# A decoder layer on Trainium2: first 128 tokens carried ahead through output projection and first queries, expert value products placed among the query blocks

## The reference

```
y_a = a_pre @ w_conv_out
y_b = attn_o @ w_attn_out
mix = sigmoid(g_a) * y_a + sigmoid(g_b) * y_b
x   = x + gate1 * (mix @ w_out)
h2  = modulate(rmsnorm(x, norm2_w), shift2, scale2)
q   = h2 @ w_q                       # 8 heads x 2 halves x 128
s   = q . sub_keys                   # 16 score rows of 128 keys
...                                  # top 16 of each half, top 16 of their 256 sums: expert numbers e
act = gelu(u_tab[e] . h2);  y = sum_k (softmax(top_s) * act)_k * v_tab[e]_k
out = x + gate2 * y
```

## Time and profile before

| what | value |
|---|---|
| median of 3 runs (lowest, highest) | 1151.59 us (1149.05, 1152.76) |
| the profiled execution | 1151.69 us |
| its span, first to last instruction | 1149.9 us |
| PE, DVE, ACT, POOL busy | 85%, 62%, 21%, 50% |
| DMA over the span | 379.89 MB, 330 GB/s |
| of it the gathers of u and v | 312.92 MB on the software queue, with the cache pages |
| first gather issued | 381.82 us |
| granted clock of TensorE, mean | 0.991 |

### The profile page before, as it was taken

The page is one execution under the profiler, slowest core; times in us unless marked ns, Lnnn a source line. Parts: engine busy times, 40 slices in busy tenths (PEclk is TensorE's granted clock), DMA queues, the critical chain, the costliest instruction groups (busy, mean ns, idle before and its releaser), DMA issues.

```text
span 1149.9 us, 10850 instructions
## 1 busy us (share of the span) xinstructions
PE 983.1 (85%) x3401; PEld 497.9 (43%) x3401; DVE 718.0 (62%) x1765; ACT 242.6 (21%) x593; POOL 575.2 (50%) x618
## 2 busy tenths in 40 slices
PE   6998889999999999998777777777777777778888
PEld 3456766667677874542232222222222222222333
DVE  2357466888644798768567467477576576444342
ACT  2111223113402133341112112121121021121111
POOL 0201001002000567777777777777777777777760
PEclk9999889999999999999999999999999999999999
DMA  9961423779537699999999999999999999999994
GB/s 314 351 221 57 152 74 129 256 256 286 148 120 287 245 345 382 409 408 410 409 409 409 409 410 409 409 409 410 410 409 409 410 409 410 409 410 409 409 411 179
DMA packets 123403, 379.89 MB, mean 330 GB/s; under 512 B 11612, under 2 KB 21080, under 8 KB 123348
## 3 DMA queue, kind: packets, MB, share of 16 engines
q0 software_dynamic: 86208, 312.92, 69.3%
q1 hardware_dynamic: 36966, 66.19, 16.7%
q10 hardware_dynamic: 174, 0.11, 0.1%
HBM read 377.59 MB, written 1.59 MB: 330 GB/s over the span
## 4 chain that ended last, share of the span: by engine, by line
PE 37%; DMA 28%; POOL 20%; issue 8%; DVE 6%; ACT 1%; SPq 0%; DVEq 0%; ACTq 0%; POOLq 0%
DMA big<-peer_v,oT 13%; POOL big L1060 9%; POOL big L1049 8%; PE twoA L567 7%; DMA big<-peer_u,oT 7%; PE twoA L880 5%; DMA r<-peer_u,oT 4%; PE twoD L935 4%; PE twoD L937 3%; PE twoD L821 3%; PE twoA L545 2%; POOL r L1049 2%; PE twoA L490 2%; PE twoD L809 1%; DMA big<-w_in 1%
## 5 line engine op out<-in xcount | busy, mean ns | idle before, releaser
L1049 POOL DMA_INDIRECT big<-peer_u,oT x230 | 216.5, 941 | 179.1 <-DVEq L1777 107.0
L1060 POOL DMA_INDIRECT big<-peer_v,oT x266 | 252.6, 950 | 87.5 <-issue 69.6
L1819 DVE CUSTOM_DVE_ANT_0 big<-big,twoA 128x1024 f32<-128x1024 f32 x128 | 156.2, 1221 | 143.5 <-DMA big<-peer_u,oT 142.5
L1819 DVE CUSTOM_DVE_ANT_0 big<-big,twoD 128x1024 f32<-128x1024 f32 x102 | 123.3, 1218 | 54.9 <-DMA big<-peer_u,oT 53.6
L935 PE MATMUL twoD<-big 128*128 128x512 f32 x176 | 97.0, 633 | 40.4 <-DMA big<-peer_v,oT 38.7
L567 PE MATMUL twoA<-hT,big 128*128 128x288 f32 x448 | 117.6, 419 | 0.0
L935 PE MATMUL twoD<-big,modT 128*128 128x512 f32 x132 | 73.1, 636 | 31.1 <-DMA big<-peer_v,oT 30.7
L567 PEld LDWEIGHTS twoA<-hT,big 128*128 128x128 f32 x448 | 86.2, 196 | 28.8 <-issue 5.9
L937 PE MATMUL twoD<-big 128*128 128x512 f32 x176 | 89.9, 592 | 0.0
L935 PEld LDWEIGHTS twoD<-big 128*128 128x128 f32 x176 | 27.5, 188 | 104.6 <-DMA big<-peer_v,oT 96.4
L935 PE MATMUL twoD<-big,rstd 128*128 128x512 f32 x90 | 49.9, 636 | 21.8 <-DMA big<-peer_v,oT 21.7
(11 more groups left out here) (368 smaller groups left out, 1419.0 us busy)
## 6 DMA issues: line engine op xcount, KB each, us to landing
big<-w_ada SPq DMA_DIRECT2D x12, 2048.0 KB, 8.3
big<-w_in SPq DMA_DIRECT2D x5, 2048.0 KB, 13.6
big<-w_in SPq DMA_DIRECT2D x9, 1024.0 KB, 7.6
big<-peer_w_q SPq DMA_DIRECT2D x3, 2048.0 KB, 8.8
big<-peer_v,oT POOLq DMA_INDIRECT x266, 18.5
big<-w_out SPq DMA_DIRECT2D x2, 2048.0 KB, 11.7
big<-peer_u,oT POOLq DMA_INDIRECT x230, 16.3
big<-w_conv_out SPq DMA_DIRECT2D x1, 2048.0 KB, 13.7
```

The lines of the kernel that those rows point to most:

```text
L1049: pool.indirect_dma_start(urows[i % NU], None, peer_u, bass.IndirectOffsetOnAxis(ap=eidx[:, t, s:s + 1], axis=0)).then_inc(u_in[i % NU], 16)
L1060: pool.indirect_dma_start(vrows[j % NV], None, peer_v, bass.IndirectOffsetOnAxis(ap=eidx[:, t, s:s + 1], axis=0)).then_inc(v_in[j % NV], 16)
L1819: dve.tensor_tensor_reduce(out=urows[i % NU], in0=urows[i % NU], in1=h2tok[t][:, :], scale=1.0, scalar=0.0, op0=ALU.mult, op1=ALU.add, acc ...
```

## The change

It reorders the second half of the mixer and the start of the expert stage.

- The first 128 columns go ahead alone. Their attention output projection stands between the sample's softmax transposes and value products (`attn_first`, 2 x 4 blocks of 128 columns, two instructions per block and k in the trace), four of their output blocks behind the value products, four behind the tail transposes, then two query blocks made together, k by k. The square sums are for 128 columns.
- The other 160 columns (`REST`) come after the first scores: `RESTS` cuts their 8 blocks in groups of 3, 3 and 2, which share PSUM banks of a new ring `R`. DVE mixes them (`rest_mix`) after `route(0)`, adds their residual at the dots 3, 6 and 8, and norms them after dot 12.
- PE makes query blocks 2 to 7 for the first 128 columns early, then 16 blocks (160 columns for the first eight, 288 for the others) with products between them: `SLOTS_BY` says how many products stand ahead of each block, 24 in all.
- The sigmoid is cut in four and stands between the key copies of ACT.
- The buffers are laid out anew: u has 6 buffers for the first 30 slots and 10 later, v has 4 for 16 slots, then 9, and 13 from slot 34 on, when the query weights are done. `w_out` goes to slots 1 and 5, the first query weights to 6. The lag grows from 14 to 20. `LATE` work moves 20 slots back.

The core of the diff (left out: the bodies that follow from the words above, such as `rest_residual`):

```diff
-        LAG, NEAR, LAST_NEAR = 18, 8, 4
+        LAG, NEAR, LAST_NEAR = 20, 14, 4
+        U_FIRST, U_ROWS = 30, 6
+        V_FIRST, V_ROWS, V_SOME = 16, 4, 34
...
-                ("out", cols(w_out, 0, 512), 5), ("out", cols(w_out, 512, 512), 6),
-                ("peerq", peer_cols(0), 5), ("peerq", peer_cols(1), 4), ("peerq", peer_cols(2), 0), ("peerq", peer_cols(3), 1)]
+                ("out", cols(w_out, 0, 512), 1), ("out", cols(w_out, 512, 512), 5),
+                ("peerq", peer_cols(0), 6), ("peerq", peer_cols(1), 4), ("peerq", peer_cols(2), 0), ("peerq", peer_cols(3), 1)]
...
         SUB_ORDER = (0, 2, 1, 3)
-        LATE = list(range(6, 6 + 2 * 15, 2))
+        LATE = list(range(26, 26 + 2 * 15, 2))
         H2_REST = 64
-        SCORE_AFTER = [4, 8, 12]
-        EARLY = {8: 0, 12: 1}
+        REST_AT, REST_NORM = (3, 6, 8), 12
+        RESTS = ((0, 3), (3, 6), (6, DC))
+        SLOTS_BY = [2 + j for j in range(8)] + [10 + 2 * j for j in range(8)]
+        SCORE_AFTER = {11: 3, 15: 4}
...
+        u_row = [i % U_ROWS if i < U_FIRST else (i - U_FIRST + U_ROWS) % NU for i in range(ROUNDS)]
+        v_some = (4, 0, 1, 2, 3, 5, 6, 7, 8)
+        v_all = (9, 10, 11, 12) + v_some
+        v_row = [j % V_ROWS if j < V_FIRST else v_some[(j - V_FIRST) % 9] if j < V_SOME else v_all[(j - V_SOME) % NV]
+                 for j in range(ROUNDS)]
+
...
+            attn_first(0)
             turn_probs(0)
             turn_probs(1)
+            attn_first(1)
             sample_values(0)
             sample_values(1)
+            pe.wait_ge(a_free, A.n)
+            sum_bank.append(bankA[(A.n + 3) % 4])
+            for j in range(4):
+                out_first(j)
...
+            for j in range(4, DC):
+                out_first(j)
...
+            first = weights(pe, group("peerq"))
+            pair = [A.open(pe) for _ in range(2)]
+            for k in range(DC):
+                pe.wait_ge(h_ready, DC + k + 1)
+                for j in range(2):
+                    mm = pe.matmul(pair[j][:, 0:P], first[:, k, j * P:(j + 1) * P], hT[:, k, 0:P], start=(k == 0), stop=(k == DC - 1))
+            A.close(mm, 2)
...
+            for j in (2, 3):
+                query(j, 0, P)
+            score_unit(1)
...
+            pe.wait_ge(oT_ready, 3)
+            w = weights(pe, group("attnout"))
+            for a, e in RESTS:
+                b = R.open(pe)
...
+                R.close(mm)
+            released[group("attnout")] = (r_full, R.n)
+            for n, (a, e) in enumerate(RESTS):
+                b = R.open(pe)
+                for j in range(a, e):
...
+                    for k in range(DC):
+                        if j == 0:
+                            pe.wait_ge(mix_ready, 3 if k < 3 else 4 if k < 6 else 5)
...
+                R.close(mm)
+            for j in (4, 5):
+                query(j, 0, P)
...
+            pe.wait_ge(sq_ready, 2 * DC + 3)
+            for c in range(DC):
...
+            rest_sum.append((a_full, A.n))
+            for j in (6, 7):
+                query(j, 0, P)
+            score_unit(2)
+            pe.wait_ge(r_free, R.n)
...
+            multiplied = 0
+            for j in range(16):
+                while multiplied < SLOTS_BY[j]:
+                    products(multiplied)
+                    multiplied += 1
+                if j == 0:
+                    pe.wait_ge(h_ready, 2 * DC + 1)
+                query(j, P if j < 8 else 0, TOK, ready=(j == 0))
+                if j in SCORE_AFTER:
+                    score_unit(SCORE_AFTER[j])
+            for j in range(multiplied, ROUNDS):
+                products(j)
...
-                if g == group("out"):
+                if g == group("out", 1):
...
                     sp.dma_start(conv_prompt, tailrows[0:2, :]).then_inc(conv_out_done, 16)
                     sp.dma_start(conv_sample.rearrange("b j c -> (b j) c"), tailrows[2:18, :]).then_inc(conv_out_done, 16)
-                if g == group("peerq", 1):
-
-                    sp.wait_ge(*released[group("out", 1)])
+                if g == group("peerq", 3):
...
+                before = row_before(u_row, i)
+                if before is not None:
+                    pool.wait_ge(u_used, before + 1)
+                elif u_row[i] >= U_ROWS:
                     pool.wait_ge(*released[group("peerq")])
-                if i >= NU:
-                    pool.wait_ge(u_used, i - NU + 1)
...
+                before = row_before(v_row, j)
+                if before is not None:
+                    pool.wait_ge(v_used, before + 1)
+                elif v_row[j] < 4:
+                    pool.wait_ge(*released[group("out", 1)])
                 else:
-                    pool.wait_ge(v_used, j - NV + 1)
...
+                    pool.wait_ge(*released[group("peerq", 1 if v_row[j] == 4 else 2 if v_row[j] < 9 else 3)])
...
-                lag = min(LAG, NEAR + 4 + i // 4, LAST_NEAR + (ROUNDS - 1 - i) // 2)
+                lag = min(LAG, NEAR + i // 6, LAST_NEAR + (ROUNDS - 1 - i) // 2)
...
+                part = sig[:, 4 * (bb - KB):4 * (bb - KB) + 4, :].rearrange("p j t -> p (j t)")
+                L.tell(act.activation(part, part, ACT.Sigmoid), gates_ready)
...
+            for j in (2, 3):
...
+            for n, (a, e) in enumerate(RESTS):
+                act.wait_ge(x1_ready, DC + n + 1)
+                L.tell(act.activation(sqR[:, a:e, :], xT[:, a:e, P:TOK], ACT.Square), sq_ready)
...
+            b = A.take(act)
+            L.tell(act.activation(rstd[:, P:TOK], b[:, 0:REST], ACT.Sqrt, bias=cv["eps"], scale=1.0 / D), sd_ready)
...
+            exps(0)
+            for j in (6, 7):
+                copy_query(j, 0, P)
+            gelus(0)
+            copy_scores()
+            act.wait_ge(h_scaled, 1)
+            for c in range(DC):
+                L.tell(act.activation(hT[:, c, P:SEQ], hT[:, c, P:SEQ], ACT.Identity, bias=modT[:, 24 + c, 0:1]), h_rest, wait=False)
...
+            made = 0
+            for j in range(16):
+                while made < SLOTS_BY[j]:
+                    diagonal(made)
+                    made += 1
+                copy_query(j, P if j < 8 else 0, TOK)
+                if j in EARLY_EXP:
+                    exps(EARLY_EXP[j])
+                if j in EARLY_GELU:
+                    gelus(EARLY_GELU[j])
+                if j in SCORE_AFTER:
+                    copy_scores()
+            for j in range(made, ROUNDS):
+                diagonal(j)
...
+            norm_scale(32, 56)
+            dve.wait_ge(gates_ready, 4)
+            dve.wait_ge(co_ready, CONV_FILL[0])
+            for i, conv_side in enumerate((bufX, bufC)):
+                L.tell(tt(sig[:, 4 * i:4 * i + 4, :], sig[:, 4 * i:4 * i + 4, :], conv_side, ALU.mult))
...
+                b = V.take(dve)
+                L.tell(dve.scalar_tensor_tensor(xT[:, j, 0:P], b[:, 0:P], modT[:, 16 + j, 0:1], xT[:, j, 0:P], ALU.mult, ALU.add),
+                       x1_ready)
+                free()
+                L.tell(ts(hT[:, j, 0:P], xT[:, j, 0:P], ab[:, j, 0:1], None, ALU.mult), wait=False)
...
+            R = Banks([bankD[0], bankD[1]], r_full, r_free)
+
+            def rest_mix(n):
+
+                a, e = RESTS[n]
+                mix(R.take(dve), a, e - a, P, TOK)
+                dve.sem_inc(r_free, 1)
...
+            for n in range(len(RESTS)):
+                rest_mix(n)
...
+                if i in REST_AT:
+                    rest_residual(REST_AT.index(i))
+                if i == REST_NORM:
+                    rest_norm()
+                if sum(chunks[weighed]) == (i + 1 if weighed >= LAST else i - 3 if weighed else i - 5):
...
+                if found < 3:
+                    steps = 2 if found == 1 or i > REST_NORM + 1 else 0
+                elif found == 3:
+                    steps = 2 if near <= 23 else 0
+                else:
+                    steps = 2 if near <= 26 else 1 if near < 44 else 0
+                for _ in range(steps):
                     if found < len(units) and next(router, True):
                         found += 1
                         router = route(found) if found < len(units) else iter(())
+                        if found <= 3:
+                            break
```

More of the change, by code:

```diff
@@ L886, in _ @@
-            score_unit(4)
+            for j in (2, 3):
[6 more added lines that the diff above has]
+                for j in range(a, e):
+                    for k in range(4):
+                        mm = pe.matmul(b[:, (j - a) * REST:(j - a + 1) * REST], w[:, k, j * P:(j + 1) * P], oT[:, k, P:TOK],
+                                       start=(k == 0), stop=(k == 3))
+                R.close(mm)
@@ L914, in late, with products @@
                     A.close(mm)
-            for j, (t, s) in enumerate(slots):
+            def products(j):
+                t, s = slots[j]
                 acc = bankD[2 * (t % 2):2 * (t % 2) + 2]
@@ L1249, in _ @@
             act.sem_inc(a_free, 1)
```

(19 more changed lines are left out.)

212 lines of the change are left out of this document (101 added, 111 removed).

## The result

The changed kernel takes 1175.2 us (median of 4 runs, 1174.0 to 1183.4), the kernel before, run beside it, 1152.0: a ratio of 1.022, with a 95% interval from 1.0195 to 1.025. It is slower, as forecast, and 8 us slower than the forecast of 1167.0: just past the 1158 to 1174 that had 0.65, and inside the 1153 to 1178 given for 8 in 10. The profiled execution took 1175.16 us, with a span of 1173.3.

What follows compares the result with a forecast made beforehand. Full DMA engines bound the kernel; a change moves only the stream's start and the idle before it is full. First gather 356.9 + idle 40 + weights 10.3 + gathers 738.4 + output 2.6 = 1148.2, forecast 1167.0 us, range 1158 to 1174 (0.65).

Steps and rivals of the forecast that it cites:

- rival C: SP's store blocks again for 8.39 us, so queries wait for weights to 350; 1175 us, chance 0.12.
- (1): Sigmoid among ACT's key copies: table load and two quarters hold up PE's first conv block by 3.8 us.
- (2): Attention projection in two halves of 3.55 us: transposes start at 309.2, second half ends at 314.9, value products at 319.4.
- (3): Output blocks, 1.78 us each plus 0.22 of square sum: four end at 327.1, four more at 336.0; first query 340.6.
- (4): SP's queue: stores issue in 0.5 us, first query weights issued at 333.0, landing 341.8; first queries start at 342.0.
- (5): First queries to first gather: 14.9 us, before 16.3; first gather at 356.9, 24.9 us earlier.
- To the first product: DVE's work between first gather and first product takes 42 us; first product at gather + 45, 16 u rows out before.
- sum 111: Query blocks, products, scores, hand-overs and table loads on PE take 111 us; last block ends at gather + 155.
- 36 + 4: DMA idle in the ramp: 36 us up to the last query block plus some 4 for refilling; 40, for 10.1 before.
- A: Faster: DVE and POOL keep the stream full, idle 10 us; 1137 us, decided at idle 25.4, chance 0.11.
- B: Half of it: idle 22 to 29 us, as hand-overs vanish or mixes fit in the first landing; near 1151, chance 0.07.
- D: TensorE's clock falls to 0.88 in the ramp, so 90 us of matmuls take 12 more; 1179 us, chance 0.05.

Runs made afterwards that it cites:

- e3: Changed kernel plus dummy work: PE multiplies constants in the two waits ahead of the first product; 1260.1 us, against 1265.1 for the changed kernel.
- e5: The changed kernel as it is, run again on what is taken to be another chip; 1265.1 us, ratio 1.024 to the kernel before.
- e2: Changed kernel with the four sigmoid quarters on ACT among the first conv copies, not the key copies; 1258.2 us, against 1265.1 for the changed kernel.

## Why the prediction was right, and what it mis-sized

The direction, the mechanism and most of the places hold; one term is too small by 8 us. That the time is also the 1175 of rival C, to 0.2 us, is chance: its mechanism didn't occur.

*The way to the first gather.* Forecast 356.9, measured 356.1. (1) The sample's scores start 4.2 us later on the chain (298.66 for 294.44 at their first long group), for 3.8. That agreement is in part luck. The first conv block starts 2.8 us later (282.82 for 280.04), although ACT's copies began 0.9 sooner (275.50 for 276.39), so the table load and two quarters cost 3.7 of the 3.8. The head start of 0.9 was in no term, and neither was a loss of 1.5: the conv blocks take 15.29 us for 13.82, at a lower clock.

Conv blocks after and before, by stretches:

```profile
282.82:298.10 15.28, 15.28 (x57) 11.50 (x58) 9.36 (x13) 6.52 (x11) 0.00 (x0) 0.90 0.82 213
280.04:293.86 13.82, 13.82 (x57) 10.56 (x58) 12.41 (x16) 4.18 (x9) 0.53 (x1) 1.00 1.04 234
```

PE had stood for 2.62 and 1.35 us just ahead of them (the wait that this step itself puts there), and the granted clock is 0.50 to 284 and 0.55 to 286. The Trainium skill (ScalarE: Activation LUTs, What ACT_TABLE_LOAD costs) would have had 5.2; ACT's row shows the activation 0.01 us behind the end of the load again, so its drain of 1.38 isn't seen here either. (2) The transposes start at 309.70 (309.2), the second half of the attention projection ends at 315.4 (314.9), the value products at 319.9 (319.4). (3) Four output blocks end at 327.5 (327.1), all eight at 336.0. (4) The query weights are issued at 332.33 (333.0) and land at 341.3 (341.8). (5) From the first queries to the gather it is 14.7 us (14.9). The stores take 0.99 and 0.98 us to issue, so rival C is out, and with it the 8.39 as a property of the store. Two halves of the attention projection were put at 0.111 us an instruction, an estimate that goes beyond its row; measured is 3.57 / 32 = 0.112.

*To the first product.* 44.4 us after the gather, for 45, and 17 u rows ahead of the first v for 16. DVE has the weights of the first product ready at 397.5, 41.5 after the gather, for 42; then ACT still has eight shifts of h2 (2.45) ahead of the diagonal. The chain runs there through the sum of squares at the low clock (386.64, 4.61 us, where e3 has 2.34 at a clock of 1.00), which no term had. So it is in part luck as well that this place comes out within a microsecond.

*The phase of query blocks.* This is the step that failed: "sum 111", the last block at gather + 155. It ends at gather + 163.0. From the timeline: blocks 8 x 2.19 + 8 x 3.89 = 48.6 (forecast 48.4), products 24 x 1.72 = 41.3 (41.3), scores 0.9 (1.9), gaps with their table loads 19.9 (19). Missing were two terms. A product behind a gap starts 0.24 us slower (1.10 for 0.86), 15 times: 3.6. And the clock: the first two products take 6.06 us for 3.68, one half product 1.48 for 0.86, one block 3.25 for 2.19, 4.1 together. The prediction had taken "two pieces of 0.86" from a product in the middle of others, though in its own schedule every block is followed by a product that starts behind a gap; the 1.10 of such a start stands in the earlier trace rows.

*The idle time.* The last of the 33 v and 54 u rows are asked by then, as forecast (87 issues up to 519). Forecast 36 + 4, measured 43.4 + 6.3: again the longer phase, and 2 in the refill, for which POOL stood 5.90 us behind the scores of the last block.

*The rivals.* A and B are out: idle 49.7, far from 25.4 (which by the prediction's own sum should be 40 - 15.3 = 24.7; nothing hangs on it). D named the right thing at the wrong size and for the wrong reason. It took the clock of a busy stretch with short gaps, 0.88, for the whole ramp, and priced 12 us. What happened is that PE stood for lack of input and ran at 1.2 GHz for a while after, in the phase (4.1 us), ahead of it (the sum of squares) and among the conv blocks (1.5); in e3, where PE hardly stood ahead of the first product, the clock stayed there. The Trainium skill (TensorE: Matmul & The Clock Gate, Part 1) ties the clock to how busy PE has been, and here the rows agree; the prediction held only the busy share of a stretch against it and not the two waits ahead of the first product, which its own step on DVE's 42 us implied.

*The signs to look for.* "DMA share near 0.75 between 357 and 512" was the wrong column: the share is 0.84 there, and the rate, 300 GB/s of 409 over 356 to 519, is 0.73. The stream is full from 535 (409 GB/s; 335 from 530 to 535), for 520.

## What to carry to other kernels

When a stream that is bound by transfers starts earlier, ask how much of other work the engine that frees its buffers must still do, and count what can be asked by the end of it: the time is the end of that work plus a nearly constant rest. There each hand-over between engines costs in full, several times over (the wait, a slower first instruction, a lower clock), so put what the next step needs in the queue ahead of what only has to be done some time. A price taken from the middle of a run of like instructions doesn't hold for one that stands alone.

## What the runs showed of the hardware

The first comparison and the later runs, by all signs on different chips of one kind, differ by 7% for this kernel: 1152 against 1231 to 1237 us for the kernel before, a full stream of 409 against 366 to 370 GB/s. In the later runs ACT, DVE and PE stand here and there for 1 to 7 us, once for 12, with their input there and nothing in the trace that they waited for (the copy at 509.80 above). This isn't scattered: e5, e3 and e2, on two chips, have the holes ahead of the same products, 7.72, 7.73 and 7.58 us, and 2.95, 2.94 and 3.00. On the first chip the same kernel has 1.11 at both places. Such stretches make an order that hands over late more expensive still. Their cause wasn't tried and stays open.

The issue of a small store on SP took 8.39 us in one kernel and 0.99 in the other, and that of the last two query weights 1.00 before and 13.41 once the gathers had begun. So it isn't set by the transfer's own size; in both cases the long one had more transfers outstanding, but no run varied that alone.
